# VectorE sums every fourth slot's value rows in a two-layer backbone with expert retrieval

## What is computed

```python
def peer(h, wq, subkeys, u_tab, v_tab):
    q = (t @ wq).reshape(-1, PEER_HEADS, 2, PEER_QDIM // 2)
    s = jnp.einsum('thpd,hpkd->thpk', q, subkeys).astype(jnp.float32)
    sv, si = lax.top_k(s, PEER_TOPK)
    cand = sv[:, :, 0, :, None] + sv[:, :, 1, None, :]
    cv, ci = lax.top_k(cand.reshape(*cand.shape[:2], PEER_TOPK * PEER_TOPK), PEER_TOPK)
    ...
    idx = i1 * PEER_KEYS + i2
    g = jax.nn.softmax(cv, axis=-1)
    def block(args):
        tb, ib, gb = args
        act = jax.nn.gelu(jnp.einsum('td,thkd->thk', tb, u_tab[ib]).astype(jnp.float32))
        return jnp.einsum('thk,thkd->td', (gb * act).astype(tb.dtype), v_tab[ib])
...
        x = x + ada_x[:, :, 5] * peer(h2, ...)
        ctx = ctx + ada_c[:, :, 5] * peer(h2c, ...)      # layer 0 only
```

## Time and profile before

| | us |
|---|---|
| median of 3 runs | 2381.09 |
| lowest and highest | 2379.73, 2384.25 |
| the profiled execution | 2382.0 |
| its span, first to last instruction | 2380.2 |
| TensorE busy | 2080.4 |
| VectorE busy | 1629.1 |
| GpSimd busy | 1021.0 |
| ScalarE busy | 961.4 |
| mean granted TensorE clock, share of full | 0.975 |

### The profile page before, as it was taken

One profiled execution on the slowest core, in us unless ns is written; L12 is line 12 of the kernel. 1 busy time (PEld: TensorE's weight loads), 2 busy tenths in 40 slices (PEclk: granted clock), 3 DMA queues, 4 the chain that ended last, 5 costly groups with the idle time before them and its releaser, 6 DMA issues.

```text
span 2380.2 us, 23945 instructions
## 1 busy us (share of the span) xinstructions
PE 2080.4 (87%) x6792; PEld 1119.3 (47%) x6792; DVE 1629.1 (68%) x3980; ACT 961.4 (40%) x2788; POOL 1021.0 (43%) x868
## 2 busy tenths in 40 slices
PE   8988998899998988988899998898799987777777
PEld 6775554455564434544454454335456532222222
DVE  2876768967766568788856668754665887766444
ACT  2113434543334444444454334534443444443333
POOL 0002444444334544444445445520233555566774
PEclk9998999999999999999999999999899999999999
DMA  9968999999999999999999999994599999999997
GB/s 402 420 252 320 394 415 421 414 422 422 421 421 421 412 421 405 421 419 420 389 406 422 421 421 421 421 381 192 224 403 379 415 421 421 422 421 421 421 421 319
DMA packets 132738, 940.46 MB, mean 395 GB/s; under 512 B 14736, under 2 KB 17936, under 8 KB 18960
## 3 DMA queue, kind: packets, MB, share of 16 engines
q0 software_dynamic: 110592, 805.36, 82.0%
q1 hardware_dynamic: 22032, 133.73, 13.7%
HBM read 937.98 MB, written 1.05 MB: 395 GB/s over the span
## 4 chain that ended last, share of the span: by engine, by line
PE 36%; DMA 29%; DVE 16%; issue 7%; POOL 6%; ACT 4%; SPq 0%; POOLq 0%; DVEq 0%; ACTq 0%
DMA uv<-uv_dram,stage_idx 28%; PE psum L948 18%; PE psum L762 9%; POOL uv L1019 6%; DVE uv L1557 6%; PE psum L744 4%; DVE h L1250 2%; PE psum L893 1%; DMA h<-c_rows_dram 1%; ACT diag L1193 1%; ACT wv L1191 1%; PE psum L680 1%; ACT gel L1189 1%; DVE work L1521 0%; PE psum L922 0%
## 5 line engine op out<-in xcount | busy, mean ns | idle before, releaser
L948 PE MATMUL psum<-uv,diag 128*128 128x512 f32 x3072 | 1449.8, 612 | 240.0 <-ACT diag L1193 221.8
L1019 POOL DMA_INDIRECT uv<-uv_dram,stage_idx x768 | 987.2, 1285 | 1051.7 <-PE psum L948 823.7
L1557 DVE CUSTOM_DVE_ANT_0 uv<-uv,h 128x1024 f32<-128x1024 f32 x768 | 935.2, 1226 | 538.1 <-DMA uv<-uv_dram,stage_idx 527.4
L948 PEld LDWEIGHTS psum<-uv,diag 128*128 128x128 f32 x3072 | 562.7, 193 | 1023.7 <-issue 518.1
L1189 ACT ACTIVATE gel<-dots 128x1 f32<-128x1 f32 x768 | 156.3, 203 | 1052.4 <-DVE dots L1557 1050.2
L1193 ACT ACTIVATE diag<-const,wv 128x128 f32<-128x128 f32 x768 | 309.8, 403 | 24.8
L762 PE MATMUL psum<-hT,wring 128*128 128x256 f32 (+1 forms) x1280 | 266.2, 362 | 1.5 <-ACT hT L1060 1.5
L762 PEld LDWEIGHTS psum<-hT,wring 128*128 128x128 f32 x1280 | 227.9, 191 | 59.7 <-issue 33.0
L1191 ACT ACTIVATE wv<-gel,gw 128x1 f32<-128x1 f32 x768 | 228.0, 297 | 25.1
L1005 POOL COPY stage_idx<-idx 128x8 uint32 (+1 forms) x96 | 33.6, 350 | 284.6 <-DVE idx L1529 283.9
L1042 ACT ACTIVATE work<-psum 128x256 f32<-128x256 f32 (+2 forms) x122 | 47.8, 393 | 137.6 <-PE psum L762 108.5
(11 more groups left out here) (216 smaller groups left out, 1289.2 us busy)
## 6 DMA issues: line engine op xcount, KB each, us to landing
uv<-ada_dram SPq DMA_DIRECT2D x25, 1024.0 KB, 17.1
wring<-in_dram SPq DMA_DIRECT2D x24, 1024.0 KB
wring<-wq_dram SPq DMA_DIRECT2D x24, 1024.0 KB
uv<-uv_dram,stage_idx POOLq DMA_INDIRECT x768
uv<-ada_t_dram SPq DMA_DIRECT2D x11, 1024.0 KB, 16.7
uv<-in_dram SPq DMA_DIRECT2D x10, 1024.0 KB, 18.9
wring<-ada_dram SPq DMA_DIRECT2D x7, 1024.0 KB
wring<-ada_t_dram SPq DMA_DIRECT2D x5, 1024.0 KB
```

Of the source, the lines that this page charges most:

```text
L948: last = mm(acc[:, b, :], diag[:, s % RING, :], uv[:, s % RING, D + 512 * b:D + 512 * (b + 1)], start=(c == 0), stop=(c == NSEL - 1))
L1019: nc.gpsimd.indirect_dma_start(out=uv[:, s, :], out_offset=None, in_=tables[stage // 2], in_offset=bass.IndirectOffsetOnAxis(ap=stage_idx[ ...
L1557: v.tensor_tensor_reduce(out=uv[:, r, 0:D], in0=uv[:, r, 0:D], in1=h2[:, row_of[stage], t, :], scale=1.0, scalar=0.0, op0=ALU.mult, op1=AL ...
```

## The change

`OWN_SUMS` names four tiles and for each a window of slots and a slot at which the sum is joined. In tile 0 it is slots 4 to 99, in tile 1 slots 60 to 77, in tile 3 slots 20 to 107, in tile 4 slots 4 to 99. Slots of the window with c%4 = 3 (`by_vector`) go another way, 24 + 4 + 22 + 24 = 74 in all; call them vector slots. Tiles 2 and 5 have none.

At a vector slot
- ScalarE leaves out `diag`,
- VectorE, at "values" s and so behind the dot of s+2, waits for `wv` and adds wv x v to a sum of its own, 1024 columns wide (`add_rows`); the first of a tile is a scaling instead,
- TensorE leaves out the two products, waits for VectorE's addition (`rows_added`) and then makes one small product of zeros into `acc`, which frees the place.

At the slots 108, 80, 114 and 108 of these tiles VectorE multiplies its sum by `gate_peer` and adds it to `x` (`join_own_sum`). The sums lie in regions that are free at that time.

```diff
--- before.py
+++ after.py
@@ -61,6 +61,20 @@
 QW = P // QUAD
 
 
+OWN_SUMS = {0: (4, 100, 108), 1: (60, 78, 80), 3: (20, 108, 114), 4: (4, 100, 108)}
+def by_vector(s):
+    T, c = s // NSEL, s % NSEL
+    return T in OWN_SUMS and OWN_SUMS[T][0] <= c < OWN_SUMS[T][1] and c % 4 == 3
+def by_tensor(s):
+    return sum(not by_vector(i) for i in range(s + 1))
 PARTS = [("ident", P), ("c", KC * 2), ("b_ada", 2 * 48), ("norm_g", 2 * 2 * KC), ("gather_sums", 4),
          ("iota", TOPK), ("cos", TT * 32), ("sin", TT * 32), ("a_conv", MC * CONV_A), ("c_conv", MC * CONV_C), ("c_conv_b", MC),
          ("c_norm_g", MC), ("vnorm_g", MIX), ("qk_g", 2 * HD), ("subln_g", P), ("lam", 4 * HD),
@@ -193,7 +207,7 @@
 DVE_TAKES = ("ac_cols", "ab_cols", "spatial", "ca_cols", "out_rows", "out_half", "out_heads")
 TAKE_AFTER = 2
 
-NEED_NONE = ("gate_diag", "mods", "lam", "v_scale", "conv", "qk_scale", "rope", "rms_root", "ada_row", *ACT_TAKES, *DVE_TAKES)
+NEED_NONE = ("own_sum", "gate_diag", "mods", "lam", "v_scale", "conv", "qk_scale", "rope", "rms_root", "ada_row", *ACT_TAKES, *DVE_TAKES)
 
 
 def needs(step, left):
@@ -267,6 +281,7 @@
     placed += spread(rms(1, (0,)) + [("norm_ctx", 2, 0)] + deal(convolve_2, heads_2) + gate(2, 0)
                      + [("out_half", 2, 0, b, t) for b in range(2) for t in range(TT)], at + 131, at + 246)
     placed += spread(gate(2, 1), 2 * STAGE_SLOTS + 40, 2 * STAGE_SLOTS + 60)
+    placed += [(T * NSEL + slot, ("own_sum", T)) for T, (_, _, slot) in OWN_SUMS.items()]
     placed.sort(key=lambda p: p[0])
 
     program, todo = [], list(placed)
@@ -492,6 +507,8 @@
         late_search = Search(h2_1, 512, (h2_1, 0), (1,))
         row_of = (0, 1, 1)
 
+        own_sum = {0: view(work, 7680, D), 1: h2[:, 1, 1, :], 3: x[:, 0, :], 4: x[:, 1, :]}
         c_rows = h2[:, 0, :, :]
         row_tmp = h2[:, 1, :, :]
 
@@ -548,7 +565,7 @@
         dots_ready, gelu_ready, wv_ready, diag_ready, uv_used = (
             sem(s) for s in ("dots_ready", "gelu_ready", "wv_ready", "diag_ready", "uv_used"))
 
-        acc_free = sem("acc_free")
+        acc_free, rows_added = sem("acc_free"), sem("rows_added")
         x_rows_ready, out_stored = sem("x_rows_ready"), sem("out_stored")
 
         program = schedule()
@@ -943,7 +960,12 @@
                 T, c = s // NSEL, s % NSEL
                 if c == 0 and T:
                     pe.wait_ge(acc_free, T)
-                pe.wait_ge(diag_ready, s + 1)
+                if by_vector(s):
+                    pe.wait_ge(rows_added, n.up("rows_added"))
+                    mm(acc[:, 0, 0:4], ident, silu_c[:, 0, 4:8], start=False, stop=False).then_inc(uv_used, 1)
+                    return
+                pe.wait_ge(diag_ready, by_tensor(s))
                 for b in range(2):
                     last = mm(acc[:, b, :], diag[:, s % RING, :], uv[:, s % RING, D + 512 * b:D + 512 * (b + 1)],
                               start=(c == 0), stop=(c == NSEL - 1))
@@ -1557,6 +1581,31 @@
                 v.tensor_tensor_reduce(out=uv[:, r, 0:D], in0=uv[:, r, 0:D], in1=h2[:, row_of[stage], t, :], scale=1.0, scalar=0.0,
                                        op0=ALU.mult, op1=ALU.add, accum_out=dots[:, r:r + 1]).then_inc(dots_ready, 1)
 
+            def add_rows(s):
+                if not by_vector(s):
+                    return
+                T, r = s // NSEL, s % RING
+                dve.wait_ge(wv_ready, s + 1)
+                rows = uv[:, r, D:2 * D]
+                if n.up(("rows", T)) == 1:
+                    done = v.tensor_scalar(own_sum[T], rows, wv[:, r:r + 1], None, ALU.mult)
+                else:
+                    dve.wait_ge(rows_added, n["rows_added"])
+                    done = v.scalar_tensor_tensor(out=own_sum[T], in0=rows, scalar=wv[:, r:r + 1], in1=own_sum[T], op0=ALU.mult, op1=ALU.add)
+                done.then_inc(rows_added, 1)
+                n.up("rows_added")
+            def join_own_sum(T):
+                stage, t = T // TT, T % TT
+                dve.wait_ge(rows_added, n["rows_added"])
+                dve.wait_ge(*taken["gate", stage, 1])
+                link(v.tensor_tensor(own_sum[T], own_sum[T], gate_peer[:, :], ALU.mult))
+                row = x[:, tile_of(stage, t), :]
+                link(v.tensor_tensor(row, row, own_sum[T], ALU.add))
+            steps["own_sum"] = join_own_sum
             def close(T):
 
                 stage, t = T // TT, T % TT
@@ -1576,7 +1625,7 @@
             v.memset(ones[:, :], 1.0)
             v.memset(silu_c[:, :, :], 0.0).then_inc(constants_set, 1)
             dve.wait_ge(const_loaded, 16)
-            walk(steps, dot, nothing, close, takes)
+            walk(steps, dot, add_rows, close, takes)
 
 
 def in_columns(w):

```

## The result

The changed kernel takes 2420.64 us (median of 4 runs, 2417.96 to 2422.18), and the kernel before 2381.32 on the same chip (4 runs, 2379.73 to 2384.25): a ratio of 1.0162 with a 95% interval of 1.0145 to 1.018. That is 39 us slower. The forecast was 2387.0 and the range ended at 2399.0, so the time lies outside the range, on the forecast's side but more than six times as far from the kernel before.

The account below looks back on a forecast made before the run. The gathers' DMA stream at 421 GB/s paces most of the span, not TensorE. Terms 0 + 0 + 4 + 2 = +6 us on the profiled 2382.0 give 2388.0, less 0.9 for the median: 2387 us, range 2371 to 2399.

Parts of the forecast that it names:

- The 19.5 us of holes beside a full TensorE: Transfer time missing against 421 GB/s where TensorE is full or nearly full, in tiles 0, 3 and 4: 19.5 us.
- the faster rival: TensorE's relief closes three quarters of the holes, tile 0's end costs 3: 2369.5 us (2365 to 2376), chance 0.18.
- The additions: VectorE's added work: 70 three-operand instructions at 1.28 us, 4 scalings and 8 join instructions, 102 us in all.
- The terms for tile 0's end and tile 4: VectorE lacks room for its additions: +4 us in tile 0, 385 to 467; +2 in tile 4, 1855 to 1970.
- The new wait: TensorE at vector slot s waits for VectorE's addition behind the dot of s+2: release 3.7 us later in quiet stretches.
- a queue that hides 7 us: In quiet stretches queued gathers let a release come 15.5 - 8.4 = 7 us late before the stream thins.
- Tile 1's four slots: The four vector slots of tile 1 were given a cost of 0.
- Tile 0 to 342, tile 4 to 1855: Stretches with TensorE's projections, where TensorE and VectorE alternate as bound: 0 together, between -17.6 and +6 us.
- The count of early and late slots: Early if TensorE's products start over 7.6 us behind the dot: about 16 of 74 save 1.5 us, others late.
- Tile 3: Stretch 1309 to 1585: VectorE has room and late releases stay within 7 us; 0, between -1.9 and +1.
- The clock rival: TensorE's gathered waits drop its clock, 1.65 us per vector slot, 12 slots unhidden: 2401 us (2394 to 2408), chance 0.12.
- The signs named: TensorE 110 us less busy, VectorE 97% and rate below 411 around 428 to 470; 421 from 215 to 342 means relief.

Follow-up runs that it names:

- relief_only: Kernel before with the 74 vector slots' products replaced by the small product, nothing added on VectorE, those rows missing from the sums: 2378.33 us, 0.9984.
- add_only: Kernel before plus VectorE's 74 additions, on constant rows into sums that nobody joins or waits for: 2388.61 us, 1.0032.
- no_wait_late: Changed kernel, but TensorE does nothing at vector slots and GpSimd's gather waits for VectorE's addition, still behind the dot of s+2: 2385.17 us, 1.0011.
- wait_only: Kernel before plus only TensorE's wait, at the 74 vector slots, for the dot two slots on: 2417.76 us, 1.0155.
- lag3_wait: Kernel before with TensorE three slots behind, not two (control, 2386.15 us), plus its wait at vector slots for the dot two slots on: 2400.49 us.
- wait_tile1: Kernel before plus TensorE's wait for the dot two slots on, at tile 1's slots 63, 67, 71 and 75 only: 2387.71 us, 1.0024.
- add_next: Changed kernel with TensorE's wait kept and VectorE's addition one slot earlier, behind the dot of s+1: 2386.28 us, 1.0019.
- no_wait: Changed kernel, but TensorE does nothing at vector slots, GpSimd waits for VectorE's addition, which stands behind the dot of s+1: 2381.65 us, 1.0003.
- warm: Changed kernel with four products of zeros, 240 columns each, on TensorE ahead of its wait at each vector slot: 2419.63 us, 1.0169.

## Why the prediction was wrong

The sign of the forecast was right and its size wrong, +6 against +39. The step that failed is the price of TensorE's new wait. By its steps:

**What bounds the kernel.** Right: the gathers' stream paces, and TensorE's time is worth little. The 19.5 us of holes beside a full TensorE, on which the faster rival lived, were no measure of what relief brings; `relief_only` got 3.5. The prediction itself had said that VectorE takes turns as the bound there.

**The additions.** Their duration was right: the three-operand form took 1.286 us where 1.28 was worked out from 480 and 747 ns, and VectorE is busy 91.9 us more, for 102 forecast. The terms for tile 0's end and tile 4, +4 and +2, make 6, and `add_only` measured 7. That they agree is partly luck, since those terms held some lateness of the wait as well. By places `add_only`'s profile, 5.0 us longer than that of before, has +4.2 in tile 0's slots 0 to 63, where the sum has nothing, +1.8 in its slots 64 to 111 and +0.9 in tile 4's slots 48 to 95.

**The new wait: the step that failed.** The prediction said that the wait decides, and then sized it as the delay of one place, "released at 908.50, 3.7 us later than now", under a queue that hides 7 us. That holds to within a few us for GpSimd (`no_wait_late`), and is wrong for TensorE, which works in order. The list gives it two slots of room over VectorE, and the steps beside the slots need that room: VectorE's part of a step waits for TensorE's, and with the change TensorE's next vector slot waits for a dot that stands behind that part. The prediction listed what is queued behind the wait, "the products of s+1 and s+2 and any projection", and put no price on it. `wait_only` puts 36 us on it, 0.5 us a slot. `lag3_wait`, with one slot more of room, takes 22 of these away; of the other 14 the cause is not separated.

**The zeros of the sum.** Tile 1's four slots, "0": +6 (`wait_tile1`). "Tile 0 to 342, tile 4 to 1855", 0 with +6 as its worst: sixteen slots of tile 0 alone take 49.1 - 44.2 = 4.9 us more, and the first 32 of tile 4 55.8 + 59.8 - 48.5 - 56.1 = 11.0. The count of early and late slots came from a trace in which TensorE was free to lie where it liked. It was not exact either: by the prediction's own test of 7.6 us, tile 4's early slots in the trace of before are 11, 15, 19, 31, 39 and 43, not those that it lists (six in both cases). The term of +4 for tile 0's end became 45.5 - 38.7 = 6.8, of which `add_only` has 3.8. Tile 3 was given 0; with the gap behind it, it takes 4.7 us more in the profile of the change, but only 1.0 in that of `wait_only`, so how much of this is the wait's is open.

**The clock rival.** Its mechanism came true: the mean granted clock fell from 0.975 to 0.939, and half-clock stretches stand in the new holes. But the losses do not follow the clock: `wait_only` lost 36 us at 0.962, `lag3_wait` 14 over its control at 0.964, `add_next` 5 at 0.953 and `no_wait` none at 0.960. By the Trainium skill ("TensorE: Matmul & The Clock Gate", "What's actually happening") the throttled clock is the default and activity lifts it; `warm`'s rise agrees. The clock's own share stays open. In the place read closely it is 7.68 - 5.32 = 2.4 us of the lump that VectorE's step waits for, and `warm`, which was to measure it, paid for its zeros about what it may have gained.

**The signs named.** The long waits of the small product, the addition's duration and GpSimd's wait came as said, and the rate from 249 to 298 did not rise to 421 but fell to 357, so by the prediction's own test the relief wasn't real. TensorE is 43 us less busy and not 110. Most of the difference is that its 694 slots take 1360.4 us, 1.96 each for 1.89 in the earlier trace rows, part of them at half clock: 694 x 0.07 = 49 us. In tile 0's end VectorE is at 42.17 of 45.50 us, 93% and not 97%: it waits too, and the rate of 321 GB/s is far below the 411 named.

## What to carry to other kernels

Where in-order engines walk one list, the distance between their parts of a slot is slack, and a wait for the other engine's newest slot spends all of it: both then take turns, though neither is full and the queue of transfers is deep. So cost a new wait not only by what it releases late but by what the waiting engine holds up for the one that it waits for. Then give the wait to the engine that needs the resource (`no_wait_late`, +3 for +39), or move the work that is waited for one slot forward (`add_next`, +5). Relief of the busiest engine should be measured by itself before a cost is accepted for it: 72 us less work brought 3.5.

## What the runs showed of the hardware

After TensorE's idle time of 6.57 us the granted clock was 0.50 of full, the level of 1.2 GHz, and again after the one of 3.93 us (stretches of after, with the columns of the earlier trace rows):

```profile
762.70:767.30 4.60, 4.60 (x7) 2.02 (x8) 3.44 (x6) 2.60 (x9) 1.55 (x2) 0.50 1.01 422
...
775.70:780.70 5.00, 5.00 (x12) 2.83 (x13) 0.60 (x2) 1.23 (x4) 1.40 (x2) 0.50 1.00 398
```

The three slots' products behind the first took 7.68 us for 5.32 in the earlier trace rows. A wait of a few microseconds thus made the work behind it slower; what this is worth in the kernel's time no run here separates. TensorE's busy time for a record of 240 columns was hardly more than that of a weight load: 132.0 / 592 = 0.22 us for 111.0 / 592 = 0.19 (`warm`).
